# Opening modulation of a two-layer backbone, computed feature block by feature block

## The chip, the core and the metric
The kernel runs on one core of a Trainium2 chip. Its engines work side by side and wait for each other by semaphores: TensorE (PE, matmuls; PEld are its weight loads), VectorE (DVE), ScalarE (ACT), GpSimd (POOL) and SyncE (SP, which here only issues DMAs). The metric is the device time of one execution in microseconds, lower is better.

## What is computed
A backbone of two layers for 512 latent and 256 context tokens of width 1024, in fp32. Only the opening of the first layer matters here:

```
sh1, sc1, ... = split(silu(c) @ w_mod[l] + b_mod[l])         # latent tokens
csh1, csc1, ... = split(silu(c_ctx) @ w_mod[l] + b_mod[l])   # context tokens
hc = rmsnorm(ctx) * (1 + csc1) + csh1
hx = rmsnorm(x) * (1 + sc1) + sh1
p = hx @ w_in[l]     # columns: q, k, v, gate, Fourier, convolution
```

Then come three token mixers (retention with decays from `ret_decay_logit`, Fourier, short convolution), an output projection, and a gated MLP with the other modulations; a last norm ends the kernel.

## The kernel before
Everything is held transposed: features on the 128 partitions, so the width of 1024 is eight feature blocks (`KB`), and the 768 tokens (`TC`) are columns. `x` holds the stream, [128, 8, 768]. A projection weight comes as a slab, a [128, 1024] tile with the eight blocks of one output column of 128. POOL splits each slab into `w_hi` and `w_lo`, the normed input is split into `h_hi` (written by ACT, which adds the shift) and `h_lo` (the rest, by DVE), and a product is three matmuls: `w_hi` with `h_hi`, `w_lo` with `h_hi`, `w_hi` with `h_lo`, each over 512 and 256 columns (`tile`, line 1005 inside `products`). Two slabs are worked on in two pairs of PSUM banks, `pair[0]` and `pair[1]`. The program is written engine by engine; each engine's order is the order of the code, and waits are explicit.

The opening of layer 0, in the order in which it hangs together:
- SP loads eight 1 MB tiles of `start_mods` (contraction block k, all 2048 columns of scale and shift, `start_slot`, line 301), with `x` in four parts between tiles 3 to 6 (line 304), then slabs 0 and 1, then tables. ACT's queue loads `c_cols` (c and c_ctx as two columns per block), `vecs`, `ident` and `small`; the last three count as first constants.
- PE, `start_mods(k)` (line 1054): `c_cols[:, k]`, two columns, is the stationary operand, and 4 x 512 columns of weights stream through it into two rows of `pair`. The sums over the eight k end with the last tile. After the seventh, `sum_squares` (line 1080) adds up the squares over the partitions.
- DVE computes the log decays of the retention (lines 638 to 650, with one Exp on ACT, line 405). ACT squares x (line 437), DVE adds the squares (line 670).
- PE spreads the reciprocal roots over the partitions (`spread_roots`, line 1100). ACT and DVE move the two rows out of PSUM (`start_rows`, lines 446 and 686), and `turn_mods` (line 1063) turns them into columns with 16 small matmuls, block 0 first. DVE adds bias and one (`first_mods`, line 693, into `modv`).
- Per block: DVE scales x (`scale`, `nt`, line 705), ACT writes `h_hi` (line 451), DVE `h_lo` (line 721); `nt` has two buffers. DVE's order is scale(0), then for each k: scale(k+1), h_lo(k).
- PE, `first_pair`: slab 0 (key block 0) and, three blocks behind, slab 1 (value block 0) follow the blocks.

Then ACT copies slab 0 to `kT` (line 475) and issues the four DMAs of its swapped rows (`rot`, line 485), DVE applies the rope (line 741) and does the dots of the other modulations (`mod_slot`, line 616), and SP's loads of the next slabs stand in one queue with the loads of `mod_slot`.

Of the kernel before, what the change touches and what calls it, by code (L numbers as in the profile page):

```python
# [18 lines left out]
P = 128  # L19
T, C = 512, 256  # L20
TC = T + C
# [15 lines left out]
SH1, SC1, G1, SH2, SC2, G2 = range(6)  # L37
Y_ORDER = [6, 7, 0, 1, 2, 3, 4, 5]
# [85 lines left out]
def build_program(nc, io):  # L124
# [26 lines left out]
    small = new("small", [P, 4])  # L151
# [17 lines left out]
    c_cols = new("c_cols", [P, KB, 2])  # L169
# [40 lines left out]
    start_slot = [at(f"start_slot{i}", [P, 2 * D], work + (8192 * i if i < 6 else 75776)) for i in range(7)]  # L210
    start_rows = at("start_rows", [2, 2 * D], work + 67584)
# [65 lines left out]
    with block:  # L277

        @block.sync
        def _(sp):  # L280
# [17 lines left out]
            for i in range(KB):  # L298
                if i == 7:
                    sp.wait_ge(start_used, 1)  # L300
                sp.dma_start(start_slot[i % 7][:, :], io["start_mods"][i, :, :]).then_inc(start_loaded[i], 16)
                if 3 <= i < 7:
                    j = i - 3
                    sp.dma_start(x[:, 2 * j:2 * j + 2, :], io["x"][:, 2 * j:2 * j + 2, :]).then_inc(x_loaded[j], 16)
            load_slab(0, 0)
            load_slab(1, 1)
            tab = io["tables"]
# [7 lines left out]
            for n_mods in MODS_KVQ:  # L315
                load_slabs(s, 1)
                if s == 2:

                    sp.wait_ge(start_turned, 2)
                    for i, name in enumerate(("c", "c_ctx")):  # L320
                        sp.dma_start(c_b[:, i, :], io[name].to_broadcast([P, D])).then_inc(c_loaded, 16)
                load_mods(m, n_mods)
                s, m = s + 2, m + n_mods
# [70 lines left out]
        def _(act):  # L394
            tab = io["tables"]
            act.dma_start(c_cols[:, :, :], io["c_cols"]).then_inc(c_cols_loaded, 16)
            for dst, src in ((vecs[:, :], io["vecs"]), (ident[:, :], tab[:, 1792:1920]), (small[:, :], tab[:, 2176:2180])):
                act.dma_start(dst, src).then_inc(first_loaded, 16)
# [5 lines left out]
            act.wait_ge(ld_ready, 1)  # L404
            nc.scalar.activation(ldt[:, 0, :], ldt[:, 1, :], ACT.Exp, scale=-1.0).then_inc(ld_ready, 1)
            act.wait_ge(ld_ready, 3)

            def decays(l):
# [4 lines left out]
                act.wait_ge(consts_loaded, 16 * (4 + l))  # L413
                for d, dst in ((0, mask), (1, eb)):
# [3 lines left out]
                for d in range(2):  # L418
                    for b in range(HB):
# [6 lines left out]
                                     scale=float(CH)).then_inc(s["decay_exp"], 1)  # L426

            def norm(name, ncol, l, sh, x_ready):
# [15 lines left out]
                if name == "n1_0":  # L444
                    act.wait_ge(start_used, KB)
                    nc.scalar.activation(start_rows[:, 0:D], pair[0][0:2, :], ACT.Copy).then_inc(start_rows_ready, 1)
                cols = [(0, 0, T)] + ([(1, T, TC)] if ncol == TC else [])
                for k in range(KB):
                    for st, a, b in cols:
                        act.wait_ge(s["nt_ready"], len(cols) * k + st + 1)  # L450
                        nc.scalar.activation(h_hi[:, k, a:b], nt[k % 2][:, a:b], ACT.Identity,
                                             bias=mod(l, st, sh, k)).then_inc(s["hi_ready"], 1)

# [8 lines left out]
            for l in range(DEPTH):  # L462
# [3 lines left out]
                if l == 0:  # L466
                    norm("n1_0", TC, 0, SH1, lambda k: act.wait_ge(x_loaded[k // 2], 16))
                else:
# [135 lines left out]
        def _(dve):  # L604
# [35 lines left out]
            dve.wait_ge(ld_ready, 2)  # L640
            chain(nc.vector.tensor_scalar(yb, ya, 2.0, None, ALU.add))
            chain(nc.vector.reciprocal(yb, yb))
            chain(nc.vector.tensor_tensor(ya, ya, yb, ALU.mult))
            chain(nc.vector.tensor_tensor(yb, ya, ya, ALU.mult))
            chain(nc.vector.tensor_scalar(yc, yb, 1.0 / 17, None, ALU.mult))
            for k in range(15, 1, -2):
                chain(nc.vector.scalar_tensor_tensor(yc, yc, 1.0 / k, yb, ALU.add, ALU.mult))
            chain(nc.vector.scalar_tensor_tensor(yc, yc, 1.0, ya, ALU.add, ALU.mult))
            chain(nc.vector.tensor_scalar(yb, lg, 0.0, None, ALU.min))
            nc.vector.scalar_tensor_tensor(ld[:, :], yc, -2.0, yb, ALU.mult, ALU.add).then_inc(ld_ready, 1)  # L650
# [22 lines left out]
            def norm(name, ncol, l, sc, sh):  # L673
# [10 lines left out]
                if name == "n1_0":  # L684
                    dve.wait_ge(start_used, KB)
                    nc.vector.tensor_copy(start_rows[:, D:2 * D], pair[1][0:2, :]).then_inc(start_rows_ready, 1)


                def first_mods(group, b0, n):

                    dve.wait_ge(start_turned, group + 1)
                    for i, one in ((b0, 1.0), (KB + b0, 0.0)):
                        nc.vector.scalar_tensor_tensor(
                            modv[:, :, i:i + n], aux(1 - group)[:, 2 * i:2 * i + 2 * n].rearrange("p (b s) -> p s b", s=2),
                            one, vecs[:, vec_at["bmod"] + i:vec_at["bmod"] + i + n].unsqueeze(1).to_broadcast([P, 2, n]),
                            ALU.add, ALU.add).then_inc(start_ready, 1)
                    dve.wait_ge(start_ready, 2 * group + 2)

                def scale(k):
                    if name == "n1_0" and k < 2:  # L700
                        first_mods(k, k, 1 if k == 0 else KB - 1)
# [29 lines left out]
            for l in range(DEPTH):  # L731
# [3 lines left out]
                norm(f"n1_{l}", TC, l, SC1, SH1)  # L735

# [260 lines left out]
        def _(pe):  # L997
# [52 lines left out]
            def start_mods(k):  # L1050

                pe.wait_ge(start_loaded[k], 16)
                for j in range(4):
                    ins = nc.tensor.matmul(pair[j // 2][0:2, j % 2 * 512:j % 2 * 512 + 512], c_cols[:, k, :],  # L1054
# [340 lines left out]
```

## Time and profile before
| | |
|---|---|
| median of 3 runs | 1671.29 us (1668.88 to 1674.12) |
| the profiled execution | 1678.89 us |
| its span, first to last instruction | 1677.0 us |
| mean granted TensorE clock | 0.976 |
| PE busy | 1600.7 us, 95% |
| DVE busy | 955.4 us, 57% |
| ACT busy | 326.3 us, 19% |
| POOL busy | 808.8 us, 48% |
| q1, the loads that SP issues | 167.79 MB |

A line of the timeline or of the chain gives start and duration in us, engine, line of the program, operation, output<-inputs, and how many instructions are merged into it. In brackets stands how long the engine had been idle before it and what released it. An fp32 matmul leaves two records (and two weight loads). PEclk is the clock granted to TensorE as a share of full speed. The whole opening is 64 of 1677 us.

### The profile page before, as it was taken

The page shows a single profiled execution, that of the slowest core. Times are in us where ns is not written, and L with a number is a line of the kernel's source. Part 1 is how long each engine was busy: PE and PEld are TensorE (multiplying, and loading weights), DVE is VectorE, ACT ScalarE, POOL GpSimd, SP SyncE. Part 2 cuts the span into 40 slices and gives each one's busy share as a digit, 9 for nine tenths or more (in the row PEclk, how much of TensorE's full clock was granted, in tenths as well). Part 3 has the DMA queues.
Part 4 walks back from the last instruction along what each step waited for, and adds up shares of the span by engine and source line. Part 5 has one row for each costly group of instructions (what it writes and reads, how often), then busy time and mean ns, then how long its engine had stood idle before and what let it go on. Part 6 is the DMA issues. An engine that isn't in the chain of part 4 may idle for free.

```text
span 1677.0 us, 24126 instructions
## 1 busy us (share of the span) xinstructions
PE 1600.7 (95%) x8780; PEld 1332.2 (79%) x8780; DVE 955.4 (57%) x1310; ACT 326.3 (19%) x489; POOL 808.8 (48%) x636
## 2 busy tenths in 40 slices
PE   8989999999989999999999999999989999999997
PEld 2878788778777888888888887877767787887876
DVE  2797554378777775874288648454456441341445
ACT  2502111221312200220022214111222220220220
POOL 1244322465334454444444443443464676666663
PEclk9899999989899999999999999999999999999998
DMA  8344111243133343332333222231122222232222
GB/s 348 119 148 150 45 51 39 85 151 113 63 116 115 118 152 113 113 137 69 107 125 113 88 98 79 83 94 51 63 88 76 89 98 88 100 100 95 93 94 94
DMA packets 49635, 174.46 MB, mean 104 GB/s; under 512 B 6448, under 2 KB 6832, under 8 KB 48560
## 3 DMA queue, kind: packets, MB, share of 16 engines
q1 hardware_dynamic: 45504, 167.79, 29.5%
q10 hardware_dynamic: 4080, 5.94, 1.4%
q8 instruction: 38, 0.62, 0.2%
q14 instruction: 13, 0.11, 0.0%
HBM read 167.41 MB, written 2.10 MB: 101 GB/s over the span
## 4 chain that ended last, share of the span: by engine, by line
PE 48%; DVE 18%; issue 14%; POOL 9%; DMA 8%; ACT 2%; DVEq 1%; ACTq 0%; SPq 0%; POOLq 0%
PE pair L1005 40%; DMA raw<-in_slabs 7%; POOL w_lo L384 5%; DVE aux L616 4%; POOL w_hi L382 3%; DVE tg L947 2%; DVE tv L947 2%; PE pair L1054 2%; DVE hid_lo L975 2%; DVE tv L972 1%; PE aux L1213 1%; DVE modv L619 1%; DVE nt L705 1%; ACT tv L586 1%; ACT hid_hi L594 1%
## 5 line engine op out<-in xcount | busy, mean ns | idle before, releaser
L1005 PE MATMUL pair<-h_hi,w_hi 128*128 128x512 f32 x1888 | 573.9, 362 | 23.1 <-POOL w_lo L384 10.9
L1005 PE MATMUL pair<-h_lo,w_hi 128*128 128x512 f32 x1888 | 566.4, 358 | 5.6 <-DVE h_lo L721 3.8
L1005 PE MATMUL pair<-h_hi,w_lo 128*128 128x512 f32 x1888 | 562.8, 356 | 0.0
L384 POOL TENSOR_TENSOR w_lo<-raw,w_hi 128x1024 fp32r<-128x1024 f32 x210 | 536.7, 2556 | 17.5
L380 POOL TENSOR_TENSOR gate<-ones 128x1 f32<-128x1 f32 x210 | 56.4, 269 | 831.3 <-PE pair L1005 736.1
L1005 PEld LDWEIGHTS pair<-h_hi,w_hi 128*128 128x128 f32 x1888 | 312.7, 191 | 81.3 <-issue 18.8
L1005 PEld LDWEIGHTS pair<-h_lo,w_hi 128*128 128x128 f32 x1888 | 311.3, 190 | 64.6 <-DVE h_lo L721 12.3
L1005 PEld LDWEIGHTS pair<-h_hi,w_lo 128*128 128x128 f32 x1888 | 312.4, 191 | 50.6
L616 DVE CUSTOM_DVE_ANT_0 aux<-mod_slot,c_b 128x1024 f32<-128x1024 f32 x160 | 235.0, 1469 | 6.1 <-DMA mod_slot<-in_mods 3.3
L382 POOL TENSOR_SCALAR w_hi<-raw 128x1024 fp32r<-128x1024 f32 x210 | 224.0, 1067 | 0.1
L911 DVE SCALAR_TENSOR_TENSOR x<-pair,modv,x 128x256 f32 (+3 forms) x96 | 60.6, 658 | 187.7 <-PE pair L1005 187.7
L1005 PE MATMUL pair<-hid_hi,w_hi 128*128 128x512 f32 (+1 forms) x528 | 161.4, 359 | 5.6 <-POOL w_lo L384 4.9
L1005 PE MATMUL pair<-hid_lo,w_hi 128*128 128x512 f32 (+1 forms) x528 | 161.1, 359 | 0.3
L1005 PE MATMUL pair<-hid_hi,w_lo 128*128 128x512 f32 (+1 forms) x528 | 160.7, 358 | 0.0
L947 DVE SCALAR_TENSOR_TENSOR tg<-pair,vecs,tg 128x511 f32<-128x511 f32 (+1 forms) x132 | 87.1, 660 | 86.7 <-ACT tg L589 78.6
L947 DVE SCALAR_TENSOR_TENSOR tv<-pair,vecs,tv 128x511 f32<-128x511 f32 (+1 forms) x132 | 87.2, 661 | 82.6 <-ACT tv L586 74.3
L1005 PEld LDWEIGHTS pair<-hid_hi,w_hi 128*128 128x128 f32 x528 | 87.6, 189 | 23.4 <-issue 6.2
L1005 PEld LDWEIGHTS pair<-hid_lo,w_hi 128*128 128x128 f32 x528 | 87.6, 189 | 17.2 <-DVE hid_lo L975 0.9
L1005 PEld LDWEIGHTS pair<-hid_hi,w_lo 128*128 128x128 f32 x528 | 87.5, 189 | 15.8
L586 ACT ACTIVATE tv<-pair,vecs 128x768 f32<-128x768 f32 (+1 forms) x44 | 35.0, 795 | 278.7 <-PE pair L1005 222.4
L975 DVE TENSOR_TENSOR hid_lo<-tv,hid_hi 128x768 f32 (+1 forms) x44 | 48.7, 1108 | 45.8 <-ACT hid_hi L594 45.8
L589 ACT ACTIVATE tg<-pair,vecs 128x768 f32<-128x768 f32 (+1 forms) x44 | 35.0, 796 | 197.2 <-PE pair L1005 197.2
(137 smaller groups left out, 1073.7 us busy)
## 6 DMA issues: line engine op xcount, KB each, us to landing
raw<-in_slabs SPq DMA_DIRECT2D x210, 512.0 KB, 3.3
mod_slot<-in_mods SPq DMA_DIRECT2D x80, 512.0 KB, 3.3
start_slot<-in_start_mods SPq DMA_DIRECT2D x8, 1024.0 KB, 13.5
x<-in_x SPq DMA_DIRECT2D x4, 768.0 KB, 18.1
rot<-kT ACTq DMA_DIRECT2D x32, 64.0 KB, 2.0
rot<-Y ACTq DMA_DIRECT2D x32, 64.0 KB, 2.1
out<-fin SPq DMA_DIRECT2D x8, 256.0 KB, 2.2
c_b<-in_c SPq DMA_DIRECT2D x1, 512.0 KB, 3.9
```

Source lines behind the costliest of these rows:

```text
L380: nc.gpsimd.tensor_tensor(gate[:, 0:1], ones[:, 0:1], ones[:, 0:1], ALU.mult).then_inc(gate_done, 1)
L382: nc.gpsimd.tensor_scalar(w_hi[p][:, :], raw[p][:, :], 1.0, 1.0, ALU.mult, ALU.mult).then_inc(split, 1)
L384: nc.gpsimd.tensor_tensor(w_lo[p][:, :], raw[p][:, :], w_hi[p][:, :].bitcast(fp32), ALU.subtract).then_inc(split, 1)
L586: nc.scalar.activation(tv[:, 0:nlat], pair[0][:, 0:nlat], ACT.Copy, scale=vec_dyn("ffnw", w))\
L589: nc.scalar.activation(tg[:, 0:nlat], pair[1][:, 0:nlat], ACT.Copy, scale=vec_dyn("ffnw", w + 3 * NHB)).then_inc(s["tg_ready"], 1)
L594: nc.scalar.activation(hid_hi[:, i, 0:nlat], tv[:, 0:nlat], ACT.Copy)\
L616: chain(nc.vector.tensor_tensor_reduce(out=aux01[:, :], in0=slab, in1=c_b[:, st, :], scale=1.0, scalar=0.0, op0=ALU.mult, op1=ALU.add, acc ...
L911: nc.vector.scalar_tensor_tensor(x[:, 2 * i + p, a0:a1], pair[p][:, a0:a1], modv[:, st, bass.ds(2 * i + (c0 + p), 1)], x[:, 2 * i + p, a0: ...
L947: ins = nc.vector.scalar_tensor_tensor(dst, src, vec_dyn("ffnw", w + tap), dst, ALU.mult, ALU.add)
L975: nc.vector.tensor_tensor(hid_lo[:, i, 0:nlat], tv[:, 0:nlat], hid_hi[:, i, 0:nlat].bitcast(fp32), ALU.subtract)\
L1005: ins = nc.tensor.matmul(out[:, a:b], wt, xt[:, a:b], start=first and k == 0, stop=last and k == 2)
L1054: ins = nc.tensor.matmul(pair[j // 2][0:2, j % 2 * 512:j % 2 * 512 + 512], c_cols[:, k, :], start_slot[k % 7][:, j * 512:j * 512 + 512], s ...
```

## The change
The weights of the opening are laid out by output block instead of contraction block: tile b holds, for all eight contraction blocks, the 128 scale and 128 shift columns of feature block b. `start_mods(b)` then makes one block's modulation alone, with eight matmuls of 256 columns. `c_cols` is widened to 32 columns, c and c_ctx first and the rest zero, and the matmuls of contraction block k write the 32 rows from 32*(k mod 4) in one PSUM bank. So four partial sums stand in four groups of 32 partitions; ACT moves all 128 rows out (`move_start_rows`), and `turn_mods(b)` adds the four up and turns them in two matmuls with two new columns of `small`. SP loads x first, slab 0 between its parts, then the tiles of the weights, in six slots instead of seven. The log decays are computed after the norm. The projection of slab 0 and 1 is interleaved with the modulation of the following blocks.

```diff
-            for i in range(KB):
-                if i == 7:
-                    sp.wait_ge(start_used, 1)
-                sp.dma_start(start_slot[i % 7][:, :], io["start_mods"][i, :, :]).then_inc(start_loaded[i], 16)
-                if 3 <= i < 7:
-                    j = i - 3
-                    sp.dma_start(x[:, 2 * j:2 * j + 2, :], io["x"][:, 2 * j:2 * j + 2, :]).then_inc(x_loaded[j], 16)
...
+            load_x(0)
+            load_x(1)
             load_slab(0, 0)
+            load_x(2)
+            load_x(3)
+            load_start(0)
+            load_start(1)
             load_slab(1, 1)
+            for b in range(2, KB):
+                load_start(b)
...
-
-                    sp.wait_ge(start_turned, 2)
...
-            act.wait_ge(ld_ready, 1)
-            nc.scalar.activation(ldt[:, 0, :], ldt[:, 1, :], ACT.Exp, scale=-1.0).then_inc(ld_ready, 1)
-            act.wait_ge(ld_ready, 3)
...
+            def move_start_rows(b):
+
+                act.wait_ge(start_used, b + 1)
+                if b >= 2:
+                    act.wait_ge(start_turned, b - 1)
+                nc.scalar.activation(start_rows[b % 2][:, :], aux(0)[:, 0:2 * P], ACT.Copy).then_inc(start_rows_ready, 1)
...
+                    if name == "n1_0" and k + 1 < KB:
+                        move_start_rows(k + 1)
...
+                def first_mods(b):
+
+                    dve.wait_ge(start_turned, b + 1)
+                    for kind, one in ((0, 1.0), (1, 0.0)):
+                        i = kind * KB + b
...
                 def scale(k):
-                    if name == "n1_0" and k < 2:
-                        first_mods(k, k, 1 if k == 0 else KB - 1)
+                    if name == "n1_0":
+                        first_mods(k)
...
                 norm(f"n1_{l}", TC, l, SC1, SH1)
+                if l == 0:
+                    log_decays()
...
+            def start_mods(b):
+
+                pe.wait_ge(start_loaded[b], 16)
+                if b:
+                    pe.wait_ge(start_rows_ready, b)
+                for k in range(KB):
+                    g = k % 4 * CG
+                    ins = nc.tensor.matmul(aux(0)[g:g + CG, 0:2 * P], c_cols[:, k, :], start_slot[b % START_SLOTS][:, k, :],
+                                           start=k < 4, stop=k >= 4)
                 ins.then_inc(start_used, 1)
...
+            def turn_mods(b):
+
+                pe.wait_ge(start_rows_ready, b + 1)
+                if b:
+                    pe.wait_ge(start_ready, 2 * b)
+                for kind in range(2):
+                    ins = nc.tensor.matmul(aux(1)[:, 4 * b + 2 * kind:4 * b + 2 * kind + 2],
+                                           start_rows[b % 2][:, kind * P:kind * P + P], small[:, 4:6], start=True, stop=True)
+                ins.then_inc(start_turned, 1)
...
+                if l == 0:
+
+                    for k in range(KB + 3):
+                        if k + 1 < KB:
+                            start_mods(k + 1)
+                        if k == 3:
+                            begin(1, 1, None)
+                        if k >= 3:
+                            tile(1, k - 3, *kv_rest)
+                        if k + 1 < KB:
+                            turn_mods(k + 1)
+                        if k == 0:
+                            begin(0, 0, None)
+                        if k < KB:
+                            tile(0, k, *kv_rest)
```

How the instructions stand on PE. Before, from the last weights of the modulation to the first block of the projection:

```order
L1054 MATMUL pair<-start_slot_112,c_cols 2x512 [waits start_mods_loaded7]
L1054 MATMUL pair<-start_slot_112,c_cols 2x512 x3
L1100 MATMUL aux<-ident,rinv 128x128 [waits rinv_ready_n1_0]
L1100 MATMUL aux<-ident,rinv 128x128 x5
L1063 MATMUL aux<-ident,start_rows 128x2 [waits start_rows_ready]
L1063 MATMUL aux<-ident,start_rows 128x2 x15
L1005 MATMUL pair<-h_hi,w_hi_54 128x512 [waits hi_ready_n1_0,slab_split]
L1005 MATMUL pair<-h_hi,w_hi_54 128x256
L1005 MATMUL pair<-h_hi,w_lo_56 128x512
L1005 MATMUL pair<-h_hi,w_lo_56 128x256
L1005 MATMUL pair<-h_lo,w_hi_54 128x512 [waits h_ready_n1_0]
L1005 MATMUL pair<-h_lo,w_hi_54 128x256
```

After, from block 1's weights to block 2's turn (line 1076 is `start_mods`, 1086 `turn_mods`, 1024 the products):

```order
L1076 MATMUL aux<-start_slot_112,c_cols 32x256 x7
L1086 MATMUL aux<-small,start_rows_118 128x2 [waits start_mods_ready,start_rows_ready]
L1086 MATMUL aux<-small,start_rows_118 128x2
L1024 MATMUL pair<-h_hi,w_hi_54 128x512 [waits hi_ready_n1_0,slab_split]
L1024 MATMUL pair<-h_hi,w_hi_54 128x256
L1024 MATMUL pair<-h_hi,w_lo_56 128x512
L1024 MATMUL pair<-h_hi,w_lo_56 128x256
L1024 MATMUL pair<-h_lo,w_hi_54 128x512 [waits h_ready_n1_0]
L1024 MATMUL pair<-h_lo,w_hi_54 128x256
L1076 MATMUL aux<-start_slot_113,c_cols 32x256 [waits start_rows_ready,start_mods_loaded2]
L1076 MATMUL aux<-start_slot_113,c_cols 32x256 x7
L1086 MATMUL aux<-small,start_rows_117 128x2 [waits start_mods_ready,start_rows_ready]
```

All modulation matmuls stood ahead of the projection; now block k+2's stand behind the `h_lo` product of block k.

On ACT, before, between the squares and the second block (`rs` are the roots):

```order
L440 ACTIVATE rs<-aux,eps 128x6 [waits sums_done_n1_0]
L446 ACTIVATE start_rows<-pair 2x1024 [waits start_weights_used]
L451 ACTIVATE h_hi<-nt_108,modv 128x512 [waits nt_ready_n1_0]
L451 ACTIVATE h_hi<-nt_108,modv 128x256 [waits nt_ready_n1_0]
L451 ACTIVATE h_hi<-nt_109,modv 128x512 [waits nt_ready_n1_0]
L451 ACTIVATE h_hi<-nt_109,modv 128x256 [waits nt_ready_n1_0]
```

And after:

```order
L457 ACTIVATE rs<-aux,eps 128x6 [waits sums_done_n1_0]
L443 ACTIVATE start_rows_117<-aux 128x256 [waits start_weights_used]
L467 ACTIVATE h_hi<-nt_107,modv 128x512 [waits nt_ready_n1_0]
L467 ACTIVATE h_hi<-nt_107,modv 128x256 [waits nt_ready_n1_0]
L443 ACTIVATE start_rows_118<-aux 128x256 [waits start_weights_used]
L467 ACTIVATE h_hi<-nt_108,modv 128x512 [waits nt_ready_n1_0]
L467 ACTIVATE h_hi<-nt_108,modv 128x256 [waits nt_ready_n1_0]
```

One copy of two long rows has become eight of 128 rows and 256 columns, each between the `h_hi` of two blocks.

## Rows read from the trace of the kernel before

**Rows 1.** Chain of waits, first 70 us: start, us, what.
```profile
6.35 25.64 PE pair L1054 x56
...
32.00 2.77 PE aux L1080 x24
...
63.94 0.82 ACT kT L475
```

**Rows 2.** DMA issues of the first 140 us: KB each, median us to landing.
```profile
vecs<-in_vecs ACTq DMA_DIRECT2D x1, 214.0 KB, 7.9
...
small<-in_tables ACTq DMA_DIRECT2D x1, 2.0 KB, 12.1
```

**Rows 3.** Stretches of the opening: busy us (x instructions) by engine, PEclk, DMA share, GB/s.
```profile
9.50:31.90 22.40, 22.40 (x53) 4.34 (x51) 9.44 (x23) 9.21 (x12) 0.00 (x0) 1.00 1.01 418
```

**Rows 4.** Timeline, all engines, 14 to 30 us: what precedes the norm.
```profile
14.39 0.19 DVE L638 TENSOR_SCALAR ldt<-vecs 128x48 f32<-128x48 f32 x1 [14.39 <-DMA small<-in_tables]
...
14.92 1.28 ACT L405 ACT_TABLE_LOAD   x1 [8.67 <-DVE ldt L639]
...
16.49 0.19 DVE L641 TENSOR_SCALAR ldt<-ldt 128x48 f32<-128x48 f32 x1 [1.67 <-ACT ldt L405]
...
20.07 0.21 DVE L650 SCALAR_TENSOR_TENSOR ld<-ldt 128x48 f32<-128x48 f32 x1
...
20.42 0.83 ACT L437 ACTIVATE sq_sum<-x 128x768 f32<-128x768 f32 x1
...
22.01 3.08 DVE L670 TENSOR_TENSOR sq_sum<-sq_sum,sq 128x768 f32<-128x768 f32 x3 [1.74 <-ACT sq L437]
...
29.13 1.58 ACT L437 ACTIVATE sq<-x 128x768 f32<-128x768 f32 x2 [2.79 <-DMA x<-in_x]
```

**Rows 5.** Timeline, all engines, 34 to 55 us: modulation, norm, first projection.
```profile
34.69 3.60 PE L1054 MATMUL pair<-start_slot,c_cols 128*2 128x512 f32 x8
...
38.33 1.01 ACT L446 ACTIVATE start_rows<-pair 2x1024 f32<-2x1024 f32 x1 [3.26 <-PE pair L1054]
...
41.32 0.23 DVE L693 SCALAR_TENSOR_TENSOR modv<-aux,vecs 128x2 f32<-128x2 f32 x2 [0.70 <-PE aux L1063]
...
45.23 0.25 DVE L693 SCALAR_TENSOR_TENSOR modv<-aux,vecs 128x14 f32<-128x14 f32 x2 [2.50 <-PE aux L1063]
...
46.30 1.12 ACT L451 ACTIVATE h_hi<-nt,modv 128x512 fp32r<-128x512 f32 x2 [2.81 <-DVE nt L705]
46.57 1.14 DVE L721 SCALAR_TENSOR_TENSOR h_lo<-nt,modv,h_hi 128x512 fp32r<-128x512 f32 x2
...
47.76 1.01 PE L1005 MATMUL pair<-h_lo,w_hi 128*128 128x512 f32 x2 [0.99 <-DVE h_lo L721]
...
48.57 0.84 PE L1005 MATMUL pair<-h_hi,w_hi 128*128 128x512 f32 x2
...
54.92 0.51 PE L1005 MATMUL pair<-h_hi,w_hi 128*128 128x512 f32 x2
...
55.27 0.51 PE L1005 MATMUL pair<-h_hi,w_lo 128*128 128x512 f32 x2
```

**Rows 6.** Stretches around the low clock, columns as in rows 3.
```profile
44.00:45.00 1.00, 1.00 (x6) 1.00 (x6) 0.00 (x0) 0.00 (x0) 0.00 (x0) 0.50 0.00 0
45.10:53.30 8.20, 7.21 (x20) 5.20 (x20) 7.93 (x17) 3.67 (x7) 0.00 (x0) 0.50 0.69 257
53.30:63.90 10.60, 10.34 (x55) 8.37 (x55) 8.76 (x17) 4.19 (x8) 0.00 (x0) 0.98 0.01 2
```

**Rows 7.** Timeline of PE, 193 to 196 us: full array, 64-column groups, full array.
```profile
193.90 1.05 PE L1213 MATMUL aux<-qxi,S_b 128*128 128x128 f32 x8
194.88 1.09 PE L1219 MATMUL aux<-St,vtok 128*64 128x128 f32 x16
195.91 0.62 PE L1005 MATMUL pair<-h_hi,w_hi 128*128 128x512 f32 x2
```

**Rows 8.** Waits of PE from 100 to 140 us: total, times, longest.
```profile
PE pair L1005 <- POOL w_lo L384: 5.3, 2, 4.6
```

## The prediction on record
> **What bounds the kernel now.** I read the chain of waits first, because the change touches only the opening of layer 0: the reader is to see that up to about 64 us there is one chain, first TensorE (PE) with the modulation matmuls from 6.35 us, then the norm, and that it ends in the first projection slab, whose copy starts at 63.94 us [rows 1]. Behind that point the edit leaves every engine its old order, so what the change is worth is read from when this copy (kT, line 475) starts. Then the timeline of the opening: which waits stand ahead of the squares, of the norm, and inside one feature block [rows 4, 5]. Then the table of stretches for the clock [rows 6]. From 45.5 us on DVE sets the pace before: modv, nt and h_lo follow each other there without a gap, and a later block, with no modv of its own, costs its nt and h_lo, 2.2 us together, while PE waits for h_lo (0.99 us at 47.76) [rows 5].
>
> **The start, by parts.** x now leads the queue and the 8 MB of weights follow. The constants gate both orders: `small` landed 12.1 us after its issue [rows 2], and DVE's first instruction stands at 14.39 behind it [rows 4]. I estimate 11.3 us for it after: `vecs`, issued two loads and 0.96 us earlier, landed after 7.9, so a load of 128 rows costs some 2.6 us, which is what its rows need if each takes turns with an 8 KB row of the weights; now the rows beside it are 6 KB (x) and 4 KB (slab 0). At 418 GB/s [rows 3] the 3.1 MB of x, slab 0 and 0.4 MB of constants need 8.8 us and are there at about 12, so ACT's waits for x (the longest 2.79 us, at 29.13 in [rows 4]) are gone. The table load costs 1.28, the probe 0.1: first square at 12.7 instead of 20.42. The log decays (16.49 to 20.28, with their Exp and its wait) leave this path. DVE's six adds run 1.03 us apart from 1.6 us behind the first square: the last ends 7.8 us behind it, at 20.5. Then, on PE:
> - sums: 2.77 us for 24 records at the high clock [rows 1]. Before, PE had been busy for 25 us; now nothing runs ahead. At the low level of the clock 6 small records took 1 us [rows 6], so 4.1.
> - block 0's weights: 8 instructions of 256 columns. Before, 8 records of 512 columns took 3.60 us with the tail [rows 5], 0.43 apart, so 16 of 256 would take 3.4 in a row. They now go to four groups of 32 array columns. What overlap does: 8 records on all 128 columns took 1.05 us (0.111 apart), 16 records on alternating halves of 64 took 1.09 (0.054 apart) [rows 7], so two groups ran fully side by side. For four I take 0.85 (1.7 at the low level) and 0.25 of tail.
> - roots: 12 records of 128 columns, at 0.111 and a tail 1.6 us at the high level, 2.8 at the low one; turning two columns and the way to DVE: 0.65 (DVE waited 0.70 for it at 41.32 in [rows 5]), 0.85 low.
> DVE's first modv comes at 20.5+2.8+0.9+1.6+0.7 = 26.5 with the high clock, at 20.5+4.1+1.7+2.8+0.9 = 30.0 with the low one. Before: 41.32 [rows 5]. So there is a head start of 11 to 15 us.
>
> **The loop, where it is given back.** The order on PE is weights(k+1), turn(k+1), then slab 0's six products of block k, the last two of which wait for h_lo(k). DVE makes h_lo(k) only behind modv(k+1) and nt(k+1), and these wait for turn(k+1). weights(k+2) stands behind the waiting product. So one block is a closed ring, with nothing of it side by side: DVE's modv, nt, h_lo and the way to PE take 2.53 (45.23 to 47.76 in [rows 5]); the h_lo product 0.35 (high) or 0.64 (high: 54.92 to 55.27; low: the pair of 48.57 has 0.84 with its tail for 0.51); weights 0.85 or 1.7; tail and ACT's copy of 128x256 to start_rows 0.25+0.42+0.1 (estimate: 1.01 us for 1024 elements, 38.33, and h_hi's 256 columns at half a microsecond); turn to DVE 0.65 or 0.85. That is 5.15 high, 6.5 low. From block 4 on slab 1's products of block k-3 stand between weights and turn, 1.05 or 1.92, in place of the copy: 5.43 or 7.65. ACT's h_hi (46.30, 1.12) is off the ring. Two changes of array shape per block cost a little more: the first record of 64 columns starts 0.20 behind the last full one instead of 0.11, and the next full one 0.21 behind the last of 64, its pair taking 0.45 for 0.35 [rows 7]; I add 0.3 per block. So 5.45 and 5.73 high, 6.8 and 7.95 low, against 2.2 before.
> The Trainium skill, page TensorEngine Tiling (Array Packing), Key Properties, says that changing the tiling mode drains TensorE. The rows show a delay of a tenth or two at each change, far under a full stop; without the rule the sum is 2 us lower. The page TensorE: Matmul & The Clock Gate (Measured speedup vs the span model) gives 3.07 for four row groups, not 4; by it a block's weights take 1.1, and the sum is some 2 us more.
>
> **The clock.** The records put the low level at 0.50 (1.2 GHz) from about 43.5 to 53.5 us, after PE had run only two-column matmuls and while it waited for nt and h_lo; it rose after the gaps had shrunk to 0.3 us, and the next 10.6 us have 0.98 [rows 6]. After the change PE does nothing until 20.5 us and then waits some 2.2 us in each block, at first with short runs between. I take the low level up to block 3, and for blocks 4 to 7, where six microseconds of work stand together, each level half the time.
>
> **Sum.** modv(0) 30.0; to modv(1) 3.6 (nothing of h_lo in it); two blocks of 6.8: 47.2; four of 6.83 (mean of 5.73 and 7.95): 74.5; from modv(7) to the end of slab 0 2.6 + 0.5 + two groups of products 3.0: 80.6, against 63.9: 16.7 us later. All high: 26.5+3.4+10.9+22.9+5.1 = 68.8, 4.9 later. All low: 30.0+3.6+13.6+31.8+7.1 = 86.1, 22.2 later.
> Other edits: the log decays on DVE (3.8 us) now lie between the last h_lo and the rope, where DVE sat idle 6.6 us for the swapped rows of kT (rows come after the copy and 4 us of issue and DMA); ACT's Exp and its table load lie in the same gap. Cost nothing; without the gap 3.8. Slots 6 and 7 of the weights wait for blocks 0 and 1 and land before 35 us, needed after 60. Slab 0 and 1 are split on POOL long ahead. c_b's and the mods' loads no longer wait for the turn, but DVE uses them only behind the rope. Silu on 256 instead of 16 elements: 0.3 us at 6 us, in which ACT is idle.
> Does the delay reach the end? The next things (rope, mod dots, the loads that wait for them, POOL's splits, PE) hang on the same copy. I take 16 us: 1678.9 of the profiled execution becomes 1694.9, and the median shown, 7.6 us lower at 1671.3, becomes 1687.3.
>
> **Rivals.**
> - The clock stays high in the whole opening: +4.9, 1676.2. For it: PE has real work in every block. Against: the low stretch above had 7.21 of 8.2 us busy.
> - The clock stays low throughout: +22.2, 1693.5; with the constants at 14.3 us as before, +25. The six microseconds of dense work speak against it.
> - The four groups don't overlap: 2.6 (high) to 5.1 us more per block, eight blocks, over +30 on the sum: above 1700. The 64-column rows speak against.
> - Part is absorbed: PE waits 5.3 us for POOL's w_lo between 100 and 140 us [rows 8]. If those waits hung on something that isn't late, +16 shrinks to +9, 1680. But slabs 4 and on are issued behind the mod loads, which wait for DVE's dots behind the rope: they move too.
> - The other side, faster: the ring is no ring because PE takes the next block's weights past the waiting product. Then a block costs modv, nt, h_hi, copy, turn: 0.26+1.91+0.45+0.75 = 3.4, slab 0 ends at 30+7x3.4+5 = 59, 5 us earlier: 1666. It decides from 4.1 us per block downward (33.9 us minus first step and tail, over six; 4.8 with the high clock). Against: h_hi of block 1 was there at 47.42, yet its products came at 48.57, behind block 0's h_lo product that started at 47.76 [rows 5]. PE keeps its order.
>
> **Numbers.** Likeliest (mixed clock) 0.62, own range 1681 to 1691; high clock 0.12; low 0.13; absorbed 0.06; no overlap 0.03; faster 0.04. No change means within 0.3%, 5 us, about what a measurement can tell. The high-clock case lies on that edge and is split: faster 0.04, same 0.08, slower 0.88. The range takes in both clock cases: 1675 to 1697.
>
> **What would show it.** In the profile after: DVE's first modv at 26 to 30 us; DVE idle over 2 us before each of the later modv, released by PE; 16 weight records in about 1.1 to 2 us; kT's copy near 80 us; everything behind it shifted alike. I am wrong if a block takes less than 4.1 us, if the 32-column records follow each other at 0.2 us, or if kT's copy moves and the end doesn't.

## The result, and the profile after
| | before | after |
|---|---|---|
| median | 1671.05 us (4 runs) | 1689.14 us (4 runs, 1685.77 to 1690.24) |
| ratio | 1 | 1.0093, 95% interval 1.0077 to 1.0109 |
| the profiled execution, its span | 1678.89, 1677.0 us | 1685.77, 1684.0 us |
| kT's copy starts | 63.94 us | 81.56 us |
| second norm's sums start (layer 0) | 417.49 us | 434.54 us |

The kernel became 18.1 us slower; 1687 was forecast, with 1675 to 1697 around it. In the experiments below one execution of the last kernel took 4804 us and one of the kernel before run beside it 2619 us; medians and ratios leave both out. The two profiled executions differ by only 6.9 us, since that of before was 8 us longer than its median: a second execution of it (below) has the first 416 us within 1.4 us of the first and the rest 10.9 us shorter. So the opening is compared by its own marks, and the effect on the time by the medians. The tail of a group of records is what its time has beyond their spacing.

The start of the opening, timeline of the kernel after, all engines; rows between these, TensorE's weight loads among them, are left out (columns as in [rows 4]):

```profile
11.61 1.28 ACT L451 ACT_TABLE_LOAD   x1 [5.54 <-DMA small<-in_tables]
...
14.61 7.07 DVE L691 TENSOR_TENSOR sq_sum<-sq_sum,sq 128x768 f32<-128x768 f32 x6 [1.07 <-ACT sq L454]
...
21.82 2.69 PE L1103 MATMUL aux<-ones,sq_sum 128*128 128x1 f32 x12 [21.82 <-DVE sq_sum L691]
...
24.37 2.70 PE L1103 MATMUL aux<-ones,sq 128*128 128x1 f32 x12
...
27.00 1.93 PE L1076 MATMUL aux<-start_slot,c_cols 128*32 128x256 f32 x16
...
28.86 2.42 PE L1123 MATMUL aux<-ident,rinv 128*128 128x128 f32 x12
...
31.56 1.07 PE L1076 MATMUL aux<-start_slot,c_cols 128*32 128x256 f32 x16
...
31.75 0.23 DVE L710 SCALAR_TENSOR_TENSOR modv<-aux,vecs 128x2 f32<-128x2 f32 x2 [4.14 <-PE aux L1086]
```

The constants arrive 2.8 us sooner than in [rows 4], the wait for x is gone, and TensorE has nothing to do before 21.82 us. The first modv stands at 31.75 against 41.32 in [rows 5]. Then the ring. One block of it, and the end of a later one, in the chain of waits of the kernel after, in which each step waits for the one above:

```profile
41.88 0.24 DVE modv L710 x2
...
42.14 1.14 DVE nt L722 x2
43.29 1.07 DVE h_lo L738 x2
...
44.40 1.01 PE pair L1024 x2
45.41 1.91 PE aux L1076 x16
47.34 0.39 ACT start_rows L443
...
47.77 1.02 PE aux L1086 x4
...
48.90 0.24 DVE modv L710 x2
...
60.40 1.00 PE aux L1076 x16
61.40 1.26 PE pair L1024 x6
62.66 0.35 PE aux L1086 x4
...
63.12 0.24 DVE modv L710 x2
```

Between the two modv no step lies beside another: 48.90 - 41.88 = 7.0 us for a block at the low clock. From block 4 on slab 1's products take the copy's place (61.40). DVE's modv stand at 31.75, 34.88, 41.88, 48.90, 57.27, 63.12, 68.96 and 76.32 us, where before a block cost 2.2. The clock in stretches (columns as in [rows 3]):

```profile
42.00:55.00 13.00, 10.21 (x50) 5.43 (x50) 4.73 (x12) 3.01 (x6) 0.00 (x0) 0.50 0.43 163
...
60.00:72.00 12.00, 8.36 (x66) 5.60 (x65) 4.85 (x12) 3.01 (x6) 0.00 (x0) 0.98 0.01 2
72.00:75.00 3.00, 3.00 (x20) 1.30 (x19) 0.00 (x0) 0.38 (x1) 0.00 (x0) 0.50 0.00 0
```

The column reads 0.50 (1.2 GHz) from about 37.4 us to 57.5, 1.00 (2.4 GHz) from 58 to 71, and 0.50 again for block 7's weights: 5.85 us per block when high, 7.0 and 8.4 (with slab 1) when low, 7.4 for the last. For the start it is of no use: it reads 1.00 from 21.8 us on, since the trace holds no record of the clock before 30.6, but up to there the durations are those of the low level. Block 0's weights take 1.93 us at 27.00, as they do later where the column reads 0.50, and block 1's 1.07 at 31.56. So where this text calls the sums, block 0's weights and the first roots low, that is read from their durations. From there to 37 us the level is high, which makes the first step, modv(0) to modv(1), 3.1 us.

### The profile page after: what moved, and what is told of

Same layout as the page of the kernel before. It is cut to its first block, busy times and chain, and to the rows that moved or that the text cites. A ratio compares the mean times of both kernels' runs of the same rounds, so it can differ in the third digit from the quotient of the medians.

```text
span 1684.0 us, 24298 instructions
## 1 busy us (share of the span) xinstructions
PE 1582.9 (94%) x8844; PEld 1333.9 (79%) x8844; DVE 956.6 (57%) x1321; ACT 328.9 (20%) x496; POOL 806.0 (48%) x636
## 4 chain that ended last, share of the span: by engine, by line
PE 48%; DVE 16%; issue 13%; POOL 9%; DMA 9%; ACT 2%; DVEq 1%; ACTq 1%; SPq 0%; POOLq 0%
PE pair L1024 41%; DMA raw<-in_slabs 8%; POOL w_lo L396 6%; DVE aux L636 3%; POOL w_hi L394 3%; DVE tg L966 2%; DVE tv L966 2%; DVE hid_lo L994 1%; DVE nt L722 1%; PE aux L1250 1%; DVE tv L991 1%; DVE h_lo L738 1%; POOL gate L392 1%; PE aux L1220 1%; ACT hid_hi L614 1%
## 5 line engine op out<-in xcount | busy, mean ns | idle before, releaser
L636 DVE CUSTOM_DVE_ANT_0 aux<-mod_slot,c_b 128x1024 f32<-128x1024 f32 x160 | 230.7, 1442 | 6.6 <-DMA mod_slot<-in_mods 3.8
```

The costliest lines, as they stand in the source:

```text
L636: chain(nc.vector.tensor_tensor_reduce(out=aux01[:, :], in0=slab, in1=c_b[:, st, :], scale=1.0, scalar=0.0, op0=ALU.mult, op1=ALU.add, acc ...
```

## Experiments
Marks in one profiled execution each, and medians; the ratio is to the kernel before, run on the same chips.

| kernel | modv(7) | kT copy | first dot of the mods | second norm | median | ratio (95%) |
|---|---|---|---|---|---|---|
| before | - | 63.94 | 73.48 | 417.49 | 1671.05 | 1 |
| before, again | - | 63.84 | 73.32 | 416.15 | 1672.54 | 1.0002 (0.9986 to 1.0018) |
| after | 76.32 | 81.56 | 91.81 | 434.54 | 1689.14 | 1.0093 (1.0077 to 1.0109) |
| after, again | 76.95 | 82.19 | 92.06 | 435.07 | 1690.60 | 1.0105 (1.0087 to 1.0123) |
| weights ahead | 61.69 | 68.39 | 77.41 | 419.07 | 1671.33 | 0.9989 (0.9976 to 1.0002) |
| one group | 100.16 | 105.45 | 115.28 | 455.52 | 1709.73 | 1.0223 (1.0197 to 1.0249) |
| decays in gap | 78.30 | 85.03 | 94.31 | 435.56 | 1688.96 | 1.0098 (1.0079 to 1.0117) |
| filler | 65.00 | 70.29 | 80.29 | 423.58 | 1677.41 | 1.0034 (1.0018 to 1.0049) |
| filler, decays in gap | 66.82 | 72.11 | 81.40 | 424.45 | 1679.57 | 1.0039 (1.0024 to 1.0054) |
| blocks ahead | 49.53 | 54.82 | 64.37 | 407.64 | 1661.55 | 0.9936 (0.9914 to 0.9959) |
| blocks ahead, filler | 49.60 | 54.89 | 64.44 | 405.21 | 1656.88 | 0.9907 (0.9891 to 0.9922) |
| the same, decays behind | 45.15 | 50.45 | 60.60 | 403.91 | 1654.42 | 0.9890 (0.9867 to 0.9913) |

From the first dot to the second norm all twelve executions take 340.2 to 344.0 us: up to there the shift of the opening is passed on within some 2 us. The median times follow the second norm less closely, between 1 us above and 4 below its shift. With the weights ahead the copy stands 4.5 us later than before and the second norm 1.6 us, yet the time is 1.9 us lower. What makes this up is open, so the marks say what an edit does to the opening, and the medians what it does to the time.

**Weights ahead.** One move in the loop on TensorE:

```diff
+                    start_mods(1)
                     for k in range(KB + 3):
-                        if k + 1 < KB:
-                            start_mods(k + 1)
...
                             turn_mods(k + 1)
+                        if k + 2 < KB:
+                            start_mods(k + 2)
```

> The changed kernel with one move on TensorE: block k+2's modulation matmuls stand right behind block k+1's turn, ahead of slab 0's products of block k, instead of behind the waiting h_lo product. Theory A (the block is a closed ring because TensorE keeps its order): weights, tail and ACT's copy leave the ring. From the changed kernel's trace a block cost 7.0 us at the low clock, 8.4 with slab 1's products, 5.85 at the high clock; now 5.2 and 7.1 low (TensorE-bound), 4.7 high. modv(7) comes near 68 us instead of 76.3, kT's copy near 74 instead of 81.6, the time falls by 7 to 8 us to about 1681. Theory B (the block is set by the way ACT -> TensorE -> DVE and its latencies, wherever the weights stand): modv(7) moves by less than 2 us and the time stays within 2 us of 1689.

Measured: modv(7) at 61.69 and the copy at 68.39, 13.2 us sooner where theory A gave 7.6. The time is 17 to 19 us lower (theory A: 7 to 8); the 4 to 6 of them that lie behind the copy stay unexplained. TensorE in one block of this kernel (timeline):

```profile
47.15 0.50 PE L1086 MATMUL aux<-small,start_rows 128*128 128x2 f32 x4
47.58 1.07 PE L1076 MATMUL aux<-start_slot,c_cols 128*32 128x256 f32 x16
48.59 0.62 PE L1024 MATMUL pair<-h_hi,w_hi 128*128 128x512 f32 x2
49.04 0.51 PE L1024 MATMUL pair<-h_hi,w_lo 128*128 128x512 f32 x2
50.28 0.61 PE L1024 MATMUL pair<-h_lo,w_hi 128*128 128x512 f32 x2 [0.73 <-DVE h_lo L738]
```

The weights now lie where TensorE waited for h_lo, and the wait left is 0.73 us. A block costs 3.6 us, with slab 1's products 4.64: the 4.7 expected at the high clock. What was not expected is the clock:

```profile
36.00:64.00 28.00, 22.07 (x184) 15.17 (x178) 16.79 (x42) 9.58 (x21) 0.00 (x0) 1.00 0.47 182
```

It stays at 2.4 GHz from 36 to 64 us; only the last block's h_lo product, behind a wait of 1.82 us, meets the low level. So the order pays twice. From modv(0) to the copy it is 49.8 us in the kernel after, 42.5 in the same order with the clock kept high (the kernel with filler, below), and 35.6 here: 7.3 us for the clock and 7.0 for the order, 1.2 us per block with slab 1 (5.85 to 4.64) and 1.8 without (5.36 to 3.59). That the shorter waits are what kept the level is seen side by side in these kernels and not tested alone. Theory B is out.

**One group.** All eight matmuls of a block in one group of 32 columns; ACT's copy and the turn read those 32 rows.

```diff
-                    g = k % 4 * CG
+                    g = 0
...
-                                           start=k < 4, stop=k >= 4)
+                                           start=k == 0, stop=k == KB - 1)
```

> The changed kernel, but all eight matmuls of a block accumulate in the same 32 array columns, so none lies beside another; ACT moves 32 rows, the turn reads 32 rows. Same results, same order. Theory A (four column groups overlap fully): a block's 16 records take 3.4 us at the high clock and 6.8 at the low one instead of 0.9 and 1.8, all of it in the ring: 20 to 30 us later at kT's copy, time 1709 to 1719; a denser TensorE may have the high clock sooner, which takes towards the low end. Theory B (the groups hardly overlap; the weight loads or the starts set the pace): under 5 us more.

Measured: 24 us later at kT's copy, 19 to 21 us in time, the low end of theory A. Timeline of TensorE:

```profile
27.30 6.01 PE L1076 MATMUL aux<-start_slot,c_cols 128*32 128x256 f32 x16
...
35.31 3.64 PE L1076 MATMUL aux<-start_slot,c_cols 128*32 128x256 f32 x16
```

3.64 us at the high level, against 1.07 in the kernel after. The 6.01 is no figure of one level: its first records start 0.43 us apart and its last 0.22, so the clock rose within it. Less the 0.25 us that I took for the tail of each, 3.39 against 0.82, that is the full factor of four; with the tail counted the quotient is 3.4.
The 3.07 that I had weighed (the Trainium skill, TensorE: Matmul & The Clock Gate, Measured speedup vs the span model) stands there for four row groups of 512 columns. These column groups gave more, 3.4 by the same kind of quotient.

**Decays in the gap.** The Exp on ACT and DVE's sixteen operations moved to behind the last square, ahead of the roots.

```diff
+                if name == "n1_0":
+                    act.wait_ge(ld_ready, 1)
+                    nc.scalar.activation(ldt[:, 0, :], ldt[:, 1, :], ACT.Exp, scale=-1.0).then_inc(ld_ready, 1)
+                    nc.scalar.activation(root_probe[:, :], eps[:, :], ACT.Sqrt)
                 act.wait_ge(s["sums_done"], 1)
...
                         add_square(name, ncol, k % 2, k)
+                    log_decays()
...
-                if l == 0:
-                    log_decays()
```

> The changed kernel with the log decays (one Exp with a table load on ACT, sixteen small operations on DVE) moved from behind the norm into the gap in which DVE and ACT wait for the sums of squares (about 21.7 to 27.1 us). In the changed kernel seven of these operations took 7.63 us beside POOL's split instead of 1.66, and the first rope began at 89.76, though kT's copy began at 81.56: 8.2 us, against 4.85 in the kernel before. Theory A (they hold up the rope): the rope begins 4.9 to 5.3 us behind the copy, near 86.7, about 3 us sooner, and the time falls by 2 to 3 us to 1686.5. Theory B (the forecast's: they cost nothing): rope earlier, but what bounds the next stage doesn't move, time within 1 us of 1689.

Measured: the time as in the kernel after (1688.96), but the profiled execution had kT's copy at 85.03, 3.5 us later. The sums began only 0.4 us later; the rest is the clock: 0.8 in the roots, at the low level to 32.9 us instead of 30.6, 0.8 in the blocks, and 1.5 behind modv(7), where a pair of records took 0.84 us instead of 0.51. So this run alone decides nothing. Hence the repeat on a kernel whose clock is steady:

**Filler.** Extra matmuls in the waits, the kernel after otherwise: two behind each of five additions of squares, three ahead of each h_lo product but the last block's. The bank that they write is overwritten before it is read.

```diff
+            def filler(n):
+                for _ in range(n):
+                    nc.tensor.matmul(aux(0)[:, 0:2 * P], x[:, 0, 0:P], x[:, 0, 0:2 * P], start=True, stop=True)
...
+                    for j in range(1, KB - 2):
+                        pe.wait_ge(norms["n1_0"]["sq_added"], j)
+                        filler(2)
                     sum_squares("n1_0", TC)
...
+                    if k == 2 and fill:
+                        filler(fill)
                     if k == 2 and lo_ready is not None:
...
-                            tile(0, k, *kv_rest)
+                            tile(0, k, *kv_rest, 3 if k < KB - 1 else 0)
```

> The changed kernel with extra matmuls whose results nobody reads, to keep TensorE busy: two of 256 fp32 columns behind each addition of squares, and three in each wait for h_lo (except the last block's). Theory A (the low clock costs what the rows show): the high level holds from before the sums on; sums 2.8 instead of 5.25 us, weights 1.0 for 1.9, roots 1.5 for 2.35, so modv(0) near 27.5 instead of 31.75; every block 5.85 instead of 7.0, 8.4 and 7.4: kT's copy near 71 to 73 instead of 81.6 and the time 8 to 10 us lower, about 1680. Theory B (the extra matmuls stand in the way as much as the clock gives, or the level doesn't rise): within 2 us of 1689 or slower.

Measured: copy at 70.29, time 1677.41, 10 to 13 us lower than after, a little more than theory A gave. The opening of this kernel (timeline of TensorE) and its clock:

```profile
22.04 1.40 PE L1110 MATMUL aux<-ones,sq_sum 128*128 128x1 f32 x12
23.30 1.48 PE L1110 MATMUL aux<-ones,sq 128*128 128x1 f32 x12
24.70 1.07 PE L1083 MATMUL aux<-start_slot,c_cols 128*32 128x256 f32 x16
25.70 1.60 PE L1130 MATMUL aux<-ident,rinv 128*128 128x128 f32 x12
```

```profile
20.00:70.00 50.00, 43.78 (x327) 32.06 (x326) 22.47 (x55) 14.56 (x28) 3.94 (x3) 1.00 0.49 199
```

Sums 2.7 instead of 5.2, modv(0) at 27.77, blocks 5.36 and 5.84. Up to the copy the low level costs the change 11 us of the 17.6: 4.0 before modv(0), 7.3 behind it. And it is the forecast's high-clock case measured: 6.4 us behind the kernel before at the copy (I had 4.9).

**Filler, decays in gap.** The move of the decays, on ACT as above and on DVE, made on the kernel with filler:

```diff
+                    log_decays()
                 dve.wait_ge(s["rs_ready"], 1)
...
-                if l == 0:
-                    log_decays()
```

> The kernel with extra matmuls in the waits (clock high in the whole opening, so that it repeats better), and the log decays moved into the gap at the sums. In the one without the move seven operations of the decays took 5.34 us beside POOL's split, and the rope began 7.9 us behind kT's copy. Theory A (they hold up the rope and what hangs on it): rope 4.9 to 5.3 us behind the copy, time 2 to 3 us lower, about 1674.5. Theory B (they cost nothing): rope sooner, time within 1 us of 1677.4.

Measured: 1679.57, not lower. From the copy to the first dot 10.0 us became 9.3; over all kernels it is 9.8 to 10.3 with the decays beside POOL's split and 9.3 to 9.6 without (9.0 with the weights ahead, where most of them were done before the split began). So behind the norm they cost some 0.6 to 1.0 us, by the pairs that differ in this alone. The move itself cost more: the sums were done sooner, DVE was still at the decays, the roots' reciprocal came at 27.34 instead of 25.11, and the copy 1.8 us later. The rope began 5.3 us behind the copy, as theory A said, but its first operation then took 2.66 us instead of 0.69, beside POOL's split. So theory A's 3 us were not there, and the time, expected by theory B within 1 us, is 2.2 us higher, with intervals that overlap.

**After and before, again.** Both without an edit, for a second profiled execution of each.

> The changed kernel as it is, once more, on the same chip as the next three, to see how far kT's copy moves from one execution to the next. Theory A (blocks pay for the level of the clock that they meet): between executions the copy may stand anywhere from about 80 to 86 us (81.56 in the first trace, 85.03 in the kernel with the decays moved), the time 1689 within 2 us. Theory B (the opening is the same in every execution, and what differs lies later): copy at 81.6 within 1 us.

Copy at 82.19, within the 1 us of theory B; but the blocks of 7.3 us lie at other places (blocks 4, 6 and 7), as theory A's mechanism has it. The sum repeats, its parts don't. The 85.03 of the decays kernel, 3.1 us of it by the clock's level at other places, speaks for theory A's range of 80 to 86, though it is another kernel.

> The kernel before as it is, once more, to see whether its opening repeats: Theory A (its TensorE work from 6 us to 38 us gives the clock the same course each time): kT's copy at 63.9 within 1.5 us, and what differs between executions (1668 to 1679 us) lies behind 400 us, where TensorE waited 7.8 us for DVE in the execution of 1678.89 us. Theory B (the clock's course differs by execution as in the changed kernel): copy off by 2 us or more.

Copy at 63.84, theory A: the difference between executions lies behind the second norm (1259.5 us from there to the end in the first, 1248.7 in this one). TensorE waited 7.8 and 3.9 us there for DVE's taps in the MLP, but most of the difference is elsewhere: it is busy for 1209.1 and 1200.3 us with the same 6394 records, and the mean granted clocks of the two executions are 0.976 and 0.981. So most of it is the level of the clock.

**Blocks ahead.** Built from what these say: blocks 0 and 1 before the sums, block 2 behind the roots, then turn(k+2) and weights(k+3) between slab 0's h_hi and h_lo products of block k, ACT's copies likewise, block 1 in a PSUM bank of its own, decays in the gap. The turn of block 0 also stands ahead of the roots, DVE takes its modv before it waits for the roots, and slab 1's products follow slab 0's. These edits were made together, so the run does not say what each gives.

```diff
+                            between = [lambda: turn_mods(k + 2)] if k + 2 < KB else []
+                            if k + 3 < KB:
+                                between.append(lambda: start_mods(k + 3))
+                            tile(0, k, *kv_rest, between)
```

> Modulation matmuls up to three blocks ahead: block 0 and 1 before the sums of squares, while TensorE waits anyway, block 2 behind the roots, then block k+3's and block k+2's turn between slab 0's h_hi and h_lo products of block k; ACT's copies of the rows likewise; log decays in the gap at the sums. Theory A (the order on TensorE is what costs, the layout by block is a gain): DVE sets 2.5 us per block or TensorE 2.7 to 3.9 at the high clock; modv(0) by 30 us, kT's copy at 56 to 60 us against 63.94 in the kernel before, time 4 to 8 us under the kernel before, about 1665. Theory B (TensorE's own work per block is the floor once the order is mended): the copy no earlier than 64 us, time that of the kernel before within 2 us.

Measured: copy at 54.82, 9.1 us sooner than in the kernel before, and the time 11 us lower; theory A had 56 to 60 and 4 to 8. In the chain of waits TensorE follows only itself:

```profile
39.15 0.34 PE aux L1093 x4
39.49 1.00 PE aux L1083 x16
40.49 1.26 PE pair L1031 x6
41.75 0.34 PE aux L1093 x4
42.09 1.00 PE aux L1083 x16
43.09 2.32 PE pair L1031 x12
```

2.6 us per block, 3.66 with slab 1, and it is busy for 22.57 of 23 us at the high clock (its stretch from 32 us on, columns as in [rows 3]):

```profile
32.00:55.00 23.00, 22.57 (x195) 16.88 (x188) 17.91 (x44) 10.05 (x22) 0.14 (x1) 1.00 0.55 213
```

The ring is gone; in the loop TensorE's own work is the bound. Theory B's floor was set too high.

**Blocks ahead, with filler; decays behind.** Four of the extra matmuls between the weights of block 0 and the sums:

```diff
+                    pe.wait_ge(x_loaded[0], 16)
                     start_mods(0)
+                    filler(1)
                     start_mods(1)
+                    pe.wait_ge(norms["n1_0"]["sq_added"], 4)
+                    filler(2)
+                    pe.wait_ge(norms["n1_0"]["sq_added"], 5)
+                    filler(1)
                     pe.wait_ge(first_loaded, 16 * 3)
```

> The kernel with the blocks ahead, plus four extra matmuls of 256 fp32 columns, whose results nobody reads, between 16 and 22 us, so that TensorE is busy nearly without a gap from 14.5 us to the sums. Theory A (the low level also costs before the first block): sums 2.8 us instead of 5.3, roots 1.6 instead of 2.4 to 2.9, modv(0) 3 to 4 us sooner, and 2 to 4 us off the time of the kernel without them. Theory B (something else, the weights' landing or ACT, sets the start): under 1 us.

Then the decays moved back behind the norm, on DVE and likewise on ACT:

```diff
-                    log_decays()
...
                 norm(f"n1_{l}", TC, l, SC1, SH1)
+                if l == 0:
+                    log_decays()
```

> The kernel with the blocks ahead and the four extra matmuls, but the log decays behind the norm again, as in the change. In the one with the decays in the gap the sums were done 3.8 us sooner by the high clock, yet TensorE then waited 2.6 us for the roots, because DVE was still at the decays until 27.4 us. Theory A (that wait ate what the extra matmuls gave, and decays behind the norm cost under 1 us): roots' reciprocal near 25, kT's copy 2 to 3 us sooner than 54.9, time 1 to 3 us lower than 1656.9. Theory B (decays beside POOL's split hold up the rope by 3 us or more and the time with it): copy sooner, time the same or up to 3 us higher.

With filler the sums take 2.7 us and end at 24.6, but the copy stays at 54.89. The line of TensorE's timeline that says why:

```profile
27.72 2.93 PE L1135 MATMUL aux<-ident,rinv 128*128 128x128 f32 x12 [2.60 <-DVE rinv L708]
```

The roots waited 2.6 us for DVE's decays, and the clock fell meanwhile (2.93 us for the roots instead of 1.6). So theory A's 2 to 4 us failed at the copy, though the sums and their clock came as it said. With the decays behind the norm the copy is at 50.45, 4.4 us sooner, more than the 2 to 3 expected. The medians (1661.55, 1656.88, 1654.42) don't follow the copies step by step. The first two differ by 4.7 us with equal copies, and the executions of the first scatter from 1656.3 to 1668.3 us. The last is 2.5 us lower, as theory A said, but its interval overlaps that of the one above it, so the times alone don't part the two. At the second norm the three stand at 407.64, 405.21 and 403.91. What takes 2.5 us between first dot and norm in the first and third more than in the second is open. The best is 1.1% under the kernel before and 2.0% under the changed one.

## Why the prediction held, step by step
- *The start.* Constants at 11.6 (11.3 forecast), x without a wait, last add at 21.7 (20.5: DVE's first operation took 1.63 us beside POOL's split of slab 0, and the last add the longest of all, 1.77, beside slab 1's). Sums 5.25 us at the low level, where I took 4.1; the level rose during the roots. modv(0) 31.75, forecast 30.0 for the low level. The head start was 9.6 us and not the 11 to 15 of the text. The 8.8 us for the loads held x and slab 0 alone (3.7 MB); with the constants it would be 9.7. No wait for x was seen, so nothing hung on it.
- *The ring.* Confirmed by its chain and by the move that opens it. Per block 7.0, 8.4 (low), 5.85 (high); forecast 6.8, 7.95 and 5.73. The terms are off both ways. In the block of 7.0 us the h_lo product took 1.01 us with its tail (0.64), the weights 1.9 (1.7), the turn 1.1 to DVE (0.85), and ACT's copy 0.4 instead of 0.8; the 0.3 for the changes of array shape is no step of its own in the chain. The bound under which the change would have been a gain is 4.0 us per block by these terms, not 4.1.
- *The four groups.* Right, 1.07 us with the tail against 1.1.
- *The clock.* Taken as low up to block 3 and half and half behind it. It was low to 30.6 us, high to 37.4, low through modv(4), and then high for two steps and low for the last. The four last steps took 27.4 us against 27.3 by the average of the two levels, and 27.8 in the second execution with another sequence: the average was right, the sequence was not foreseen. That the low level costs 11 us was within the two sums (22.2 - 4.9 = 17.3 for all).
- *The sum.* kT's copy at 81.56 against 80.6; 17.6 us later against 16.7. It is this close partly by luck: modv(0) came 1.75 us later than forecast, the next step 0.5 sooner, the two behind it 0.4 later, the last four as forecast, and the end from modv(7) to the copy took 5.2 us instead of 6.1.
- *Decays at no cost.* Nearly: 0.6 to 1.0 us. The cover that I named (6.6 us of idle DVE) was there, but POOL's split lies in it, which I had not seen: seven operations took 7.63 us.
- *Passed on to the end.* 18.1 by the medians for 17.6 at the copy; nothing absorbed. In the other kernels time and copy part by up to 7 us, so this closeness is worth less than it looks.
- *The median of the runs shown* as a base was right, and the profiled execution of before no measure of the whole.

What was not in the forecast: how strongly the level of the clock hangs together with the length of the waits. It made the one move worth 13 us at the copy and not 7.6.

## What to carry to other kernels
Cutting a serial stage into blocks gains only if the next block's first step does not stand, on any engine, behind this block's last wait: write down one block as a list of who waits for whom, add it up, and compare with the slowest engine's own share. Here the sum was 5.9 to 8.4 us, the slowest engine's share 2.6 to 3.7, and looking two or three blocks ahead on the same layout turned a loss of 18 us into a gain of 11, or 16 to 17 with extra matmuls. In a kernel's first microseconds it also pays to keep TensorE at 2.4 GHz, since sums, roots and turns all cost more at 1.2; extra matmuls in the waits did it here, 31 on the order of the change and four with the blocks ahead. Waits are not all that counts: in the kernel before the level fell at about 43.4 us, though TensorE had run its two-column turns without a pause, and stayed low to 53.5 us [rows 6].

## What the runs showed of the hardware
- Matmuls on four groups of 32 array columns ran side by side at the full factor: 16 fp32 records of 256 columns in 1.07 us, against 3.64 in one group.
- Changing between column groups and the full array in each block cost little: in the kernel with the blocks ahead the first product's pair behind the weights is followed by the next after 0.46 us (35.22 to 35.68), a later one after 0.36 (35.68 to 36.04). The weights start 0.43 us behind a turn (36.39 to 36.82), a product 0.36 (48.91 to 49.27). The Trainium skill (TensorEngine Tiling (Array Packing), Key Properties) says that a change of tiling mode drains TensorE; by these rows that is about a tenth of a microsecond at each change.
- Small matmuls pay for the clock too: 24 records of one column took 5.25 us in the kernel after, 2.7 where extra matmuls ran ahead of them; the kernel before has 2.77 [rows 1].
- Small DVE operations can take as long as a POOL operation beside which they run. Timeline of DVE and POOL in the kernel after:

```profile
81.50 7.63 DVE L668 SCALAR_TENSOR_TENSOR ldt<-ldt 128x48 f32<-128x48 f32 x7
...
82.94 2.38 POOL L396 TENSOR_TENSOR w_lo<-raw,w_hi 128x1024 fp32r<-128x1024 f32 x1
```

Seven operations of 48 columns, 1.66 us when POOL is idle, took 7.63; in the chain single ones have 2.45 and 2.31 us, as long as one w_lo.
